# Layer 0 of a two-layer decoder trunk: six of the twenty pieces of the input projection computed from split weights

## The reference

```
h = rmsnorm(x, norm1_g[l]) * (1.0 + sc1) + sh1
z = h @ w_in[l]                                   # 1024 -> 2560
u_a, v_a, q_b, k_b, v_b = jnp.split(z, splits, axis=-1)
out_a = gmlp_mixer(u_a, v_a, ...)                 # gelu(u) * (W_s @ norm(gelu(v)) + b)
out_b = diff_attention(q, k, v, lam, ...)         # 4 heads, two softmax maps each
y = jnp.concatenate([out_a, out_b], axis=-1) @ w_out[l]
x = x + g1 * y
```

## Time and profile before

| | us |
|---|---|
| median of 3 runs | 1259.88 |
| lowest and highest of them | 1259.84, 1260.71 |
| the profiled execution's own time | 1260.55 |
| its span | 1258.1 |
| TensorE busy | 1219.8 (97%) |
| VectorE busy | 1082.7 (86%) |
| ScalarE busy | 836.3 (66%) |

### The profile page before, as it was taken

How to read it: one execution, slowest core, us unless ns; L and a number is a source line. 1 busy time by engine, 2 the same in 40 slices (tenths; PEclk the granted TensorE clock), 3 DMA queues, 4 the chain that set the end, 5 groups by cost and what they waited for, 6 DMA issues and landing times.

```text
span 1258.1 us, 17137 instructions
## 1 busy us (share of the span) xinstructions
PE 1219.8 (97%) x5374; PEld 856.7 (68%) x5374; DVE 1082.7 (86%) x1312; ACT 836.3 (66%) x1093; POOL 55.1 (4%) x71
## 2 busy tenths in 40 slices
PE   6999999999989999999999999999999999999997
PEld 2445667777767776776776776776776776776765
DVE  4677898788889878998998998998998998998997
ACT  3125554444455658777777777777777777777875
POOL 1102100000000202000000000000000000000000
PEclk9999999999999999999999999999999999999999
DMA  9998858898859446999999999999999999999980
GB/s 350 358 387 287 262 184 300 286 322 289 315 199 334 136 167 258 384 388 357 385 389 346 383 389 344 386 389 347 386 389 347 385 389 344 385 389 345 400 308 33
DMA packets 196238, 409.59 MB, mean 326 GB/s; under 512 B 6708, under 2 KB 45628, under 8 KB 195940
## 3 DMA queue, kind: packets, MB, share of 16 engines
q1 hardware_dynamic: 192100, 393.82, 85.8%
q0 software_dynamic: 4096, 15.25, 3.7%
HBM read 401.70 MB, written 7.34 MB: 325 GB/s over the span
## 4 chain that ended last, share of the span: by engine, by line
PE 84%; DVE 10%; issue 2%; ACT 2%; DMA 1%; SPq 1%; DVEq 0%; ACTq 0%
PE bank L2025 22%; PE bank L2026 22%; PE bank L2027 22%; PE bank L2186 5%; PE bank L2032 3%; PE bank L2036 2%; PE bank L2033 2%; DVE ada_acc L1388 2%; DVE w_lo L1336 2%; DVE more_lo L1336 1%; DMA raw<-in_w_ada 1%; PE bank L2520 1%; PE bank L2063 1%; ACT more_hi L857 1%; SPq L666 1%
## 5 line engine op out<-in xcount | busy, mean ns | idle before, releaser
L1336 DVE TENSOR_TENSOR w_lo<-raw,w_hi 128x1024 fp32r<-128x1024 f32 x366 | 440.3, 1223 | 59.0 <-ACT w_hi L857 56.8
L857 ACT ACTIVATE w_hi<-raw 128x1024 fp32r<-128x1024 f32 x366 | 383.5, 1058 | 131.7 <-PE bank L2027 116.1
L1336 DVE TENSOR_TENSOR more_lo<-raw,more_hi 128x1024 fp32r<-128x1024 f32 x264 | 315.2, 1219 | 13.9 <-ACT more_hi L857 13.3
L857 ACT ACTIVATE more_hi<-raw 128x1024 fp32r<-128x1024 f32 x264 | 276.4, 1061 | 60.1 <-PE bank L2027 60.1
L2025 PE MATMUL bank<-w_hi,hgT_hi 128*96 128x512 f32 x352 | 140.3, 399 | 0.3 <-DVE w_lo L1336 0.3
L2026 PE MATMUL bank<-w_hi,hgT_lo 128*96 128x512 f32 x352 | 139.1, 395 | 0.0
L2027 PE MATMUL bank<-w_lo,hgT_hi 128*96 128x512 f32 x352 | 138.1, 392 | 0.0
L1388 DVE SCALAR_TENSOR_TENSOR ada_acc<-raw,silu_c,ada_acc 128x512 f32<-128x512 f32 x152 | 114.7, 755 | 18.3 <-DMA raw<-in_w_ada 11.5
L2025 PE MATMUL bank<-more_hi,hgT_hi 128*96 128x512 f32 x320 | 127.3, 398 | 1.2 <-DVE more_lo L1336 1.2
L2026 PE MATMUL bank<-more_hi,hgT_lo 128*96 128x512 f32 x320 | 126.4, 395 | 0.0
L2027 PE MATMUL bank<-more_lo,hgT_hi 128*96 128x512 f32 x320 | 125.4, 392 | 0.0
(11 more groups left out here) (334 smaller groups left out, 1757.5 us busy)
## 6 DMA issues: line engine op xcount, KB each, us to landing
raw<-in_moe_w_gate SPq DMA_DIRECT2D x88, 1024.0 KB, 8.9
raw<-in_moe_w_up SPq DMA_DIRECT2D x88, 1024.0 KB, 9.3
raw<-in_moe_w_down SPq DMA_DIRECT2D x88, 1024.0 KB, 10.0
raw<-in_w_ada SPq DMA_DIRECT2D x48, 1024.0 KB, 11.1
raw<-in_w_in SPq DMA_DIRECT2D x20, 1024.0 KB, 11.6
raw<-in_ffn_w_gate SPq DMA_DIRECT2D x11, 1024.0 KB, 5.5
raw<-in_ffn_w_up SPq DMA_DIRECT2D x11, 1024.0 KB, 8.0
raw<-in_ffn_w_down SPq DMA_DIRECT2D x11, 1024.0 KB, 11.0
```

What stands on the lines that cost most here:

```text
L857: act.activation(like(hi_of(s)), src, ACT.Copy).then_inc(hi_done, 1)
L1336: dve.tensor_tensor(like(lo_of(s)), src, like(hi_of(s).bitcast(F32)), ALU.subtract).then_inc(split_done, 1)
```

## The change

Pieces 8 to 13 of layer 0, the whole value block and the first half of the gate block, are made from split weights in three passes; the other fourteen pieces stay plain. For that:

- ScalarE rounds the rows `hT` into two new tiles `in_rows_hi` (one for each half of the depth) and VectorE takes the differences into `hT_lo`, in piece 2. `in_rows_hi` lies in `z[:, half, 0:1024]`, the columns of u and gate.
- ScalarE does `split_hi` and VectorE `split_lo` for the six pieces, each in its own piece of the loop, ahead of the other work that stands there on VectorE and behind it on ScalarE.
- The slots of the three chunks come free at the split.
- ScalarE copies the value block out of PSUM (after the exponentials of head 0, in piece 14) and the gate block (before the exponentials of head 3, in piece 18); VectorE's two copies are gone in layer 0.
- Because the map of head 1 is written where `in_rows_hi` lies, ScalarE waits in piece 15, ahead of the exponentials of head 1, until TensorE has used all six split pieces.

```diff
+FIRST_SPLIT = range(8, 14)
+FIRST_DONE = [2, 4, 4, 5, 7]
...
-    DIRECT = [c[0] == "in" and c[1] == 0 for c in STREAM]
+    DIRECT = [c[0] == "in" and c[1] == 0 and 4 * IN_ORDER.index(c[2]) + 2 * c[3] not in FIRST_SPLIT for c in STREAM]
...
+        in_rows_hi = [sb(f"in_rows_hi{half}", [P, KT // 2, SEQ], F32R, offset=zbase + half * INW * 4) for half in range(2)]
...
                 if i == 0 and piece == 2:
+                    act.wait_ge(tr_mm, 4)
+                    rows_in_hi(0)
                     transposed(0, 1)
+                    rows_in_hi(1)
+
+            def rows_in_hi(half):
+
+                act.wait_ge(tr_hi, 2 * half + 2)
+                act.wait_ge(tr_lo, 2 * half + 2)
+                act.activation(in_rows_hi[half][:, :, :], hT[:, 4 * half:4 * half + 4, :], ACT.Copy).then_inc(in_hi_done, 1)
...
+                    if layer == 0 and piece == 15:
+                        act.wait_ge(split_used, S_IN[0] + len(FIRST_SPLIT))
                     if piece in (14, 15):
                         exponentials(piece - 14)
+                    if piece == 14 and layer == 0:
+                        evacuate(V_AT, v_out)
                     if piece == 17:
                         exponentials(2)
                     if piece == 18:
+                        if layer == 0:
+                            evacuate(G_AT, g_out)
                         exponentials(3)
...
-                    if layer and piece > 2:
+                    if piece in FIRST_SPLIT or layer and piece > 2:
                         in_hi(layer, piece)
...
                     transposed(0, 1)
+                    for half in range(2):
+                        dve.wait_ge(in_hi_done, half + 1)
+                        dve.tensor_tensor(hT_lo[:, 4 * half:4 * half + 4, :], hT[:, 4 * half:4 * half + 4, :],
+                                          in_rows_hi[half][:, :, :].bitcast(F32), ALU.subtract).then_inc(in_lo_done, 1)
...
-                    if piece == 14 and layer == 0:
-                        copy_block(V_AT, v_out)
-                    if piece == 18:
+                    if piece == 18 and layer:
                         copy_block(G_AT, g_out)
-                    if layer and piece > 2:
+                    if piece in FIRST_SPLIT or layer and piece > 2:
                         in_lo(layer, piece)
...
                     pe.wait_ge(split_done, taken(WHERE[("in", layer, IN_ORDER[t], sub // 2)], sub % 2))
+                    if layer == 0:
+                        pe.wait_ge(in_lo_done, 2)
...
+                        rows_hi_of = hT_hi[:, k, :] if layer else in_rows_hi[k // 4][:, k % 4, :]
...
-                    if layer == 0:
+                    if not is_split(layer, piece):
...
-                    elif piece > 2:
+                    elif layer == 0 or piece > 2:
```

More of the change, by code:

```diff
@@ L160, in trunk @@
     S_IN = [0, 0]
-    S_OUT = [0, 0]
+    S_OUT = [len(FIRST_SPLIT), 0]
     S_FFN = S_OUT[0] + 4 * (D // CB)
@@ L166, in trunk, with in_split, is_split @@
     assert EXPERT_SPLITS % NB_MOE == 0 and NB_MOE == 2 * NB
+    def in_split(layer, piece):
+        return S_IN[layer] + piece - (0 if layer else FIRST_SPLIT[0])
+    def is_split(layer, piece):
+        return layer == 1 or piece in FIRST_SPLIT
     def split_in_block(b, q):
@@ L443, in trunk @@
         in0_used = sem("in0_used")
+        in_hi_done = sem("in_hi_done")
+        in_lo_done = sem("in_lo_done")
         q_out = sem("q_out")
@@ L971, in in_hi @@
                 wait_chunk("in", n)
-                split_hi(S_IN[layer] + piece, raw[:, n % RING, q * SUB:(q + 1) * SUB], flat)
+                split_hi(in_split(layer, piece), raw[:, n % RING, q * SUB:(q + 1) * SUB], flat)
             def gu_hi(b, q):
@@ L1010, in block_done @@
                 def block_done(t):
-                    if layer == 0:
-                        act.wait_ge(in0_used, 2 * (t + 1))
+                    if is_split(layer, 4 * t + 3):
+                        act.wait_ge(split_used, in_split(layer, 4 * t + 4))
                     else:
-                        act.wait_ge(split_used, S_IN[layer] + 4 * (t + 1))
+                        act.wait_ge(in0_used, FIRST_DONE[t])
                 def evacuate(t, signal):
@@ L1487, in in_lo @@
                 n = WHERE[("in", layer, j, half)]
-                split_lo(S_IN[layer] + piece, taken(n, q), raw[:, n % RING, q * SUB:(q + 1) * SUB], flat)
+                split_lo(in_split(layer, piece), taken(n, q), raw[:, n % RING, q * SUB:(q + 1) * SUB], flat)
             def gu_lo(b, q):
@@ L1510, in block_done @@
                 def block_done(t):
-                    if layer == 0:
-                        dve.wait_ge(in0_used, 2 * (t + 1))
+                    if is_split(layer, 4 * t + 3):
+                        dve.wait_ge(split_used, in_split(layer, 4 * t + 4))
                     else:
-                        dve.wait_ge(split_used, S_IN[layer] + 4 * (t + 1))
+                        dve.wait_ge(in0_used, FIRST_DONE[t])
                 def copy_block(t, signal):
@@ L2189, in split_piece @@
                 def split_piece(piece, t, sub, a, rows=None):
-                    s = S_IN[layer] + piece
+                    s = in_split(layer, piece)
                     pe.wait_ge(split_done, taken(WHERE[("in", layer, IN_ORDER[t], sub // 2)], sub % 2))
+                    if layer == 0:
+                        pe.wait_ge(in_lo_done, 2)
                     products = []
@@ L2196, in split_piece @@
                         cols = slice(CB * kk, CB * kk + CB)
-                        products.append((in_bank(t, a)[:, :], hT_hi[:, k, P * a:P * a + P],
+                        rows_hi_of = hT_hi[:, k, :] if layer else in_rows_hi[k // 4][:, k % 4, :]
+                        products.append((in_bank(t, a)[:, :], rows_hi_of[:, P * a:P * a + P],
                                          hT_lo[:, k, P * a:P * a + P], hi_of(s)[:, cols], lo_of(s)[:, cols],
```

## The result

The changed kernel takes 1265.34 us (median of 6 runs, 1264.31 to 1267.69) against 1260.14 of the kernel before (6 runs): a ratio of 1.004, 95% interval 1.003 to 1.005, 5.2 us slower. The span of its profiled execution is 1263.6 us, 5.5 more than before. The loss is made in one place, between 75 and 105 us, and is carried to the end unchanged.

What follows compares the result with a forecast made beforehand. TensorE bounds layer 0's input projection, meeting VectorE's queue at piece 14. A 2.5 us later start there plus 1.5 us of clock loss gives 4.0 us, so a median of 1263.9 us, range 1261.6 to 1267.2.

Steps and rivals of the forecast that it cites:

- Split pieces: Layer 0 pieces 8 to 13 on TensorE: 2.81 us each instead of 3.44, 3.8 us over the six.
- Work ahead of piece 8: Piece 2, around 43 us: two ScalarE copies and two VectorE subtractions cost nothing; uncovered they would be 2.4 us.
- The wait on the keys: Before the scores, after pieces 8 and 9: TensorE waits about 1.4 us for VectorE's keys copy, until 75.6.
- End of piece 13: TensorE in layer 0: piece 13 ends at 92.11, 2.38 us earlier than before.
- ScalarE's wait and the tail: Ahead of piece 14: head 1's exponentials wait for piece 13; TensorE idles 5.4 us, starting 2.5 us later than before.
- VectorE there in time: At head 1's maps: VectorE's own way ends at about 91.3, before ScalarE's exponentials end at 93.85.
- second rival: Piece 14: ScalarE's wait doesn't bind, VectorE alone sets the start; not slower, 1258.7 or 1259.9; chance 0.10.
- The clock: After the gap ahead of piece 14: TensorE's granted clock falls, costing 1.5 us, with 0 and 3.0 as ends.
- The copies: ScalarE's value copy runs before TensorE needs its bank; after piece 14, gate copy and VectorE's relief neither cost nor give.

## Why the prediction was right, step by step

The direction and each link of the mechanism came as forecast. The median was forecast at 1263.9 and is 1265.34, inside the range; the move is 5.2 us instead of 4.0.

- **Split pieces.** Forecast 2.81 us each. Pieces 10 to 12 take 78.75 to 87.19, 2.81 each.
- **Work ahead of piece 8.** Forecast as hidden. VectorE's two subtractions end at 45.18, and it still waits 2.00 us for the chunk that lands at 47.18.
- **The wait on the keys.** Forecast 1.4 us and scores from 75.6; it was 1.58 and 75.78. The run with the earlier copy shows that it is worth this much at the meeting point.
- **End of piece 13.** Forecast 92.11; 92.34.
- **ScalarE's wait and the tail.** Exponentials forecast from 92.14, 1.71 us long; 92.38 and 1.72. From the first instruction of the maps to TensorE forecast 3.66 us; 94.19 to 97.86 is 3.67. So the gap was 5.52 for 5.4 and the late start 2.82 for 2.5.
- **VectorE there in time.** Forecast ready at about 91.3 with a wait of 1.1 us for ScalarE's part of piece 13. It waited 1.75 us for that and was ready at 91.65, 2.54 us before ScalarE. The second rival therefore had its point right: with ScalarE's wait gone, VectorE sets the meeting point, and TensorE resumes near the time before (0.96 us later in one execution, 0.05 in another), not earlier.
- **The clock.** This is the term that was mis-sized: "Part of the low stretch will fall into the gap itself, so I take 1.5 us for it, with 0 and 3.0". It measured 2.61 in the profiled execution, and filling the gap brought the difference to the kernel before from 5.2 to 2.8 us. The forecast took the 1.70 us lost in layer 1 and put part of that low stretch into the gap. Part did fall there, from about 96.3 to 97.86, but the stretch was twice as long as in layer 1: it went on to about 103.2, so the matmuls that resumed at 97.86 ran at half rate for 5.3 us.
- **The copies.** "Neither is on the chain" was said of what comes after piece 14, and holds for the gate copy. For the value copy the forecast was right that ScalarE is in time for TensorE's bank; it did not say how much VectorE would have cost there, 1.77 us of waiting at piece 12.

What stays open is how the clock's share varies from run to run. The changed kernel's runs spread over 3.4 us, the map elsewhere without filling over 8.6, and only one execution of each was profiled, so where the clock fell in the others is not known. A second thing is open, which the forecast did not have: in the nine executions with split pieces TensorE waits 0.23 to 1.72 us for a chunk of weights at 44 us, in the three without at most 0.17. In the changed kernel's it is 0.24, so it has next to no part in the 5.43 us; whether the split pieces cause it is not shown.

## What to carry to other kernels

Before making one engine faster, look for the next place where it meets another engine's queue. Here 3.8 us of shorter passes could not be kept: even with the map put elsewhere TensorE met VectorE no earlier than before (95.09 against 95.04), and the return of a borrowed buffer put ScalarE, then VectorE, then TensorE itself behind the last short pass. A wait that costs 0.55 us today is worth checking for whether it has to stand where it does: it guarded a bank that is first written again two pieces later, and moving it turned 5 us of loss into a gain of 1.5. And a gap in TensorE's work is to be priced with the clock behind it, which here nearly doubled its cost.

## What the runs showed of the hardware

The same gap does not always lower the clock. Layer 1 has an idle stretch of 2.58 to 2.60 us in each of the twelve profiled executions; the granted clock falls after it in ten and stays at 1.00 in two. Nor is the price the same: the fall costs 1.7 us of full-rate work in nine of the ten and 3.4 in one, the run with the keys earlier and the gap filled. In the run with the wait at piece 14 left out, the stretch of 10 us around it shows no fall:

```profile
426.05 0.50 PE L2055 MATMUL bank<-w_hi,hT_hi 128*128 128x512 f32 x1 [2.59 <-DVE z L1553]
```

```profile
425.00:435.00 10.00, 8.95 (x47) 7.60 (x48) 8.04 (x13) 8.95 (x21) 5.22 (x4) 1.00 0.17 67
```

The idle stretch that ends at 16 us, a wait for a load, lowers it in four of the twelve, where it was 2.94 to 3.48 us long; in the other eight it was 1.73 to 2.86. The wait for the keys lowered it where it was 2.15 us long, and not where it was 1.15 to 1.58. So a difference of 1 to 2 us between two single executions of this kernel may be the clock alone, and the times of many runs are needed for a verdict.
